# A fused two-block transformer kernel: moving operands at 128 instead of 256 modulo 512 bytes

## The reference

```python
def first_block(x, ...):
    z = rms_norm(h, attn_norm) @ w_in
    h = h + concat([gated_linear_attention(z), softmax_attention(z)]) @ w_out
    h = h + square(relu(rms_norm(h, mlp_norm) @ w_mlp_up)) @ w_mlp_down      # 1024 x 4096, 4096 x 1024
    return h + (p @ w_ple_proj) * sigmoid(rms_norm(h, ple_norm) @ w_ple_gate + b)

def second_block(x, ...):
    for i in range(2):
        h = rmsnorm(x, mix_norm[i])
        x = x + (pool_mixer(h) if i == 0 else chunk_attention(h))
        h = rmsnorm(x, ffn_norm[i])
        x = x + (silu(conv3(h @ w_gate[i])) * (h @ w_val[i])) @ w_out[i]     # 1024 x 2816 twice, 2816 x 1024
```

## The kernel before, in words

| tiles | before | after |
|---|---|---|
| X | 256 | 256 |
| AH (37,632 before), AL | 256 | 128 |
| RAW | 256 | 128 |
| WH (86,784 before), WL, stage, sq, rb, t2s | 256 | 256 |
| HH, HL (from 149,760 before) | 256 | 128 |
| OH, OL, OM, LM, pH, pL, cqb, v2, qTa, kTa | 256 | 256 |
| TH, TL, GH, GL | 448 | 448 |
| cst (with the identity) | 128 | 128 |

## Time and profile before

### The profile page before, as it was taken

How to read it: one execution, slowest core, us unless ns; L and a number is a source line. 1 busy time by engine, 2 the same in 40 slices (tenths; PEclk the granted TensorE clock), 3 DMA queues, 4 the chain that set the end, 5 groups by cost and what they waited for, 6 DMA issues and landing times.

```text
span 1613.5 us, 21756 instructions
## 1 busy us (share of the span) xinstructions
PE 1605.2 (99%) x9056; PEld 1357.5 (84%) x9056; DVE 1105.1 (68%) x1700; ACT 762.3 (47%) x1131; POOL 116.0 (7%) x102
## 2 busy tenths in 40 slices
PE   9999999999999999999999999999999999999999
PEld 7877878898989888888899898877777788899897
DVE  6798664696757657887587577546655877587575
ACT  5476445444443446654155244456565634155241
POOL 1300000011111100000000000312201200000000
PEclk9999999999999999999999999999999999999999
DMA  5310328356464521223222223322221213223222
GB/s 189 107 49 28 105 79 122 83 113 139 87 139 85 139 104 53 79 79 131 79 105 110 100 92 117 129 82 100 78 77 53 79 52 131 79 105 112 98 92 91
DMA packets 28065, 156.09 MB, mean 97 GB/s; under 512 B 3712, under 2 KB 5392, under 8 KB 12096
## 3 DMA queue, kind: packets, MB, share of 16 engines
q1 hardware_dynamic: 26352, 149.75, 25.8%
q0 software_dynamic: 1328, 4.86, 5.6%
q10 hardware_dynamic: 288, 0.10, 0.0%
HBM read 149.98 MB, written 4.72 MB: 96 GB/s over the span
## 4 chain that ended last, share of the span: by engine, by line
PE 95%; DVE 2%; ACT 1%; POOL 0%; DMA 0%; issue 0%; SPq 0%; DVEq 0%; ACTq 0%
PE bank L885 20%; PE bank L887 20%; PE bank L886 20%; PE bank L891 3%; PE bank L1494 3%; PE bank L1496 3%; PE bank L1495 3%; PE bank L893 3%; PE bank L892 3%; PE bank L1343 2%; PE bank L1345 2%; PE bank L1344 2%; PE bank L1611 1%; PE bank L1140 1%; PE bank L1621 1%; PE bank L1637 1%
## 5 line engine op out<-in xcount | busy, mean ns | idle before, releaser
L2152 DVE TENSOR_TENSOR WL<-RAW,WH 128x2048 fp32r<-128x2048 f32 (+2 forms) x90 | 199.6, 2224 | 129.8 <-ACT WH L1680 129.8
L885 PE MATMUL bank<-AH,WH 128*128 128x512 f32 (+1 forms) x718 | 283.2, 394 | 0.2 <-DVE X L2182 0.2
L887 PE MATMUL bank<-AH,WL 128*128 128x512 f32 (+1 forms) x718 | 279.7, 390 | 0.0
L886 PE MATMUL bank<-AL,WH 128*128 128x512 f32 (+1 forms) x718 | 279.6, 389 | 0.0
L885 PE MATMUL bank<-HH,WH 128*128 128x512 f32 x608 | 236.6, 389 | 0.0
L886 PE MATMUL bank<-HL,WH 128*128 128x512 f32 x608 | 236.6, 389 | 0.0
L887 PE MATMUL bank<-HH,WL 128*128 128x512 f32 x608 | 236.5, 389 | 0.0
L1680 ACT ACTIVATE WH<-RAW 128x2048 fp32r<-128x2048 f32 (+2 forms) x90 | 165.9, 1854 | 118.2 <-PE bank L887 81.5
L885 PEld LDWEIGHTS bank<-AH,WH 128*128 128x128 f32 (+1 forms) x718 | 134.4, 187 | 30.3 <-issue 2.4
L887 PEld LDWEIGHTS bank<-AH,WL 128*128 128x128 f32 (+1 forms) x718 | 134.4, 187 | 29.0
L886 PEld LDWEIGHTS bank<-AL,WH 128*128 128x128 f32 (+1 forms) x718 | 134.5, 187 | 28.0 <-issue 1.0
(11 more groups left out here) (389 smaller groups left out, 3262.9 us busy)
## 6 DMA issues: line engine op xcount, KB each, us to landing
RAW<-in_W SPq DMA_DIRECT2D x124, 1024.0 KB, 4.8
RAW<-in_W SPq DMA_DIRECT2D x9, 768.0 KB, 4.5
X<-in_XT SPq DMA_DIRECT2D x16, 256.0 KB, 5.3
ev_scratch<-ev POOLq DMA_DIRECT2D x16, 160.0 KB, 7.6
Gb<-ev_scratch SPq DMA_DIRECT2D x16, 128.0 KB, 4.3
Gb<-ev_scratch SPq DMA_DIRECT2D x16, 112.0 KB, 3.9
out<-X SPq DMA_DIRECT2D x7, 256.0 KB, 2.0
RAW<-in_W SPq DMA_DIRECT2D x2, 512.0 KB, 5.3
```

The costliest lines, as they stand in the source:

```text
L885: e.matmul(o, a, h, start=first, stop=False)
L886: e.matmul(o, a, l, start=False, stop=False)
L887: return e.matmul(o, c, h, start=False, stop=last)
L2152: e.tensor_tensor(k.WL[j][:, 0:n], k.RAW[RAW_OF[u]][:, 0:n], k.WH[j][:, 0:n].bitcast(F), SUB).then_inc(*WLO.mark(u))
```

## The change

Before AH the allocator now skips 384 bytes, so that AH and AL lie at 128 modulo 512, and so does RAW behind them; WH is brought back to 256 with `in_step`. The second stage's HH and HL start 128 bytes ahead of a place that is 256 modulo 512. The small tile `bps` moves into the gap behind `t1s`, and the `band` tiles keep their places relative to HH. TH, TL, GH and GL stay where they are. No instruction, wait or transfer is added, removed or moved in order.

```diff
+BEHIND = 384
@@ memory
     k.X = a.tile("X", [P, 8, S])
+    a.at += BEHIND
     k.AH = a.tile("AH", [P, 8, S], R)
     al_at = a.at
     k.AL = a.tile("AL", [P, 8, S], R)
     raw_at = a.at
     k.RAW = [a.tile(f"RAW{i}", [P, UE]) for i in range(NR)]
-    wh_at = a.at
+    wh_at = a.at = in_step(a.at)
     k.WH = [a.tile(f"WH{i}", [P, UE], R) for i in range(NW)]
...
-    a.at = base
+    hh_at = a.at = base + BEHIND - 512
     k.HH = [a.tile(f"HH{i}", [P, S], R) for i in range(NH)]
     k.HL = [a.tile(f"HL{i}", [P, S], R) for i in range(NH)]
     k.t1s = [a.tile(f"t1s{i}", [P, S + 2]) for i in range(2)]
+    k.bps = a.tile("bps", [P, 8])
     inner = a.at = in_step(a.at)
...
-    k.bps = a.tile("bps", [P, 8])
...
-              enumerate([base + 4 * S * 8] + [base + 4 * S * (NH + 8) + 4 * 4 * BW * i for i in range(3)])]
+              enumerate([hh_at + 4 * S * 8] + [hh_at + 4 * S * (NH + 8) + 4 * 4 * BW * i for i in range(3)])]
```

## The result

The changed kernel takes 1642.35 us (median of 4 runs, 1641.35 to 1644.11) against 1615.11 us before (median of 4): a ratio of 1.0164, 95% interval 1.0151 to 1.0176. It is slower, by 27 us; I had forecast 1579 us. The profiled execution took 1644.11 us, its span is 1641.9 us, and its mean granted clock is 0.997, against 1.000 before. It is the longest of the four; the spans of the others were 1639.2, 1639.3 and 1641.0 us.

What follows compares the result with a forecast made beforehand. TensorE, busy 99% of the span, bounds the kernel through its pitch per matmul. Gains of 33.4 + 6 = 39.4 us, less 8%, leave 36 us: 1615.2 - 36 = 1579 us, own range 1571 to 1588, whole range 1560 to 1617.

Steps and rivals of the forecast that it cites:

- (e): RAW at 128, so ScalarE and VectorE mix places within an instruction: 0, both engines having spare time.
- (f): Transfers into RAW start at another place: 0, ScalarE's waits for them not being on TensorE's path.
- The reading of the surplus: Weight load and moving stream conflict in SBUF: 32 cycles per matmul at the same place, at most 16 at 192 bytes.
- (a): 3978 matmuls of 512 columns with AH, AL, HH or HL moving: pitch 226.7 to 218.3 ns, gain 33.4 us.
- (b): 1104 matmuls of 256 columns with AH or AL moving: gain 6 us, 7.4 at most.
- (c): 672 value-projection matmuls with AH stationary, distance +128: taken as 0, between -4.5 and +4.5 us.
- (d): TH, TL, GH, GL, OH, OM, pH and cqb keep their distance: 0.
- The 8% taken off for VectorE: Deducted from TensorE's 39.4 us gain, as VectorE is nearly full in one stretch and 5% of the chain isn't TensorE.
- The slower one: Rival: longer conflict at -128, 560 cycles instead of 544; (a) costs +26.6 us, (b) +7.4, giving 1649 us; 14%.
- Its mechanism: Slower rival's reason: at -128 the faster moving stream starts behind the load, catches up and crosses it in full.
- The repetition rival: Places repeat every 128 bytes, so 384 equals 0: surplus stays 32 cycles, 1615 us; 13% together with the ports' rule.
- 73% for faster: Chance of a gain over 3.2 us: forecast case 48% plus the floor case 25%.

Runs made afterwards that it cites:

- the bench: Kernel of nothing but fp32r matmuls at many places, reference computation left out: 512 columns 226.8 ns at distance 0, 233.3 at 192; 256 columns 120.0 and 113.4.
- e2: Changed kernel with AH, AL, RAW, HH and HL at 448 modulo 512, weights still at 256: 1638.63 us, ratio 1.0146 to the kernel before.
- e4: Changed kernel with AH, AL, RAW, HH and HL at 0 modulo 512, weights at 256: 1616.26 us beside 1616.45 for the kernel before, ratio 1.0001.
- b3: Matmuls alone, other types, one repeated operand pair, and different preceding blocks: 512 columns bf16 215.8 or 215.9 ns, float32 429.2; 256 fp32r columns 113.3 or 117.8.

## Why the prediction was wrong

**What bounds the kernel.** Right. TensorE's pitch is the time; no other engine, wait or transfer took part in the result, and (e) and (f) were 0 as costed.

**The reading of the surplus.** Here it failed. From three sizes at distance 0 I had a surplus of 32 cycles, the same at 256, 384 and 512 columns, and concluded that it belongs to the weight load. Then I took TH's 16 cycles, measured with 256 columns at distance 192, as the upper end for distance -128 with 512: the sum's 5.0 ns in (a) is the middle between it and float32's 3.3. Neither row was a bound. With 256 columns a gain of 6.7 ns at distance 192 is real; with 512 the same distance loses 6.5 ns (226.8 against 233.3), and from 320 columns on no distance went under 13.3. At the change's own distance, 128, the surplus with 512 columns is 19.1 to 20.0 ns (232.4 and 233.3). Constant in the columns at one distance did not mean constant at another, and even at distance 0 three sizes were too few: 448 columns cost 16.0. And float32, at half the rate, has no trouble with any distance, so it says nothing of fp32r.

**(a)** was +23.1 us (11.8 + 11.3) in place of -33.4. **(b)** was 0.0 in place of -6; the bench at -128 gives 118.7 ns where TH's place gives 113.4. **(c)** was +3.0, within its bounds of 4.5 but not 0: the exchanged sides pay as the others do. **(d)** held for the places: 101 OH and OL matmuls are 227.1 ns apart in the trace after, though e2 showed that a tile can change its pitch without being moved. The 8% taken off for VectorE had no occasion to show itself.

**The rivals.** The slower one came true, at 14%, in sign and nearly in size: it priced (a) at +26.6 us for 560 cycles and the matmuls measured 233.3 ns at one place and 232.9 on average. Its +7.4 for the 256-column forms did not come, and (c) did, so 1649 became 1642. Its mechanism is not supported: it turned on the sign of -128, and +128 costs as much. So the price came out nearly right for a reason that did not hold, which is luck. The repetition rival was right in form and wrong in period: the pattern repeats every 256 bytes (e4), not every 128. Because 384 is 128 modulo 256, the change leaves the one good place; a step of 256 would have been free.

**The two rules.** The Trainium skill's page "TensorE: Matmul & The Clock Gate", under "Step-by-step: what each phase is for", gives the moving operand and the weights read ports of their own, and by that no distance can matter. bf16 and float32 agree with it in b3, to 0.1 ns; fp32r does not, by up to 11 ns. The same page's "Back-to-back issue gap" gives N/2.4 + 2.5 ns for a warm matmul alone, by estimate 215.8 ns for 512 columns; bf16 measured 215.8 and 215.9, fp32r 226.7 at the best.

**The numbers.** 73% for faster was too much for a quantity of which no row had either the distance or the size. An honest pair of ends for (a) would have reached as far above 13.3 ns as below.

What stays open is the cause beneath the distance. The surplus doesn't scale with the stationary columns, one displaced operand in four disturbs the whole triple, and two rhythms occur at the same places. A conflict between stream and load with some fixed slot in it would fit, but no run here shows it.

## What to carry to other kernels

For fp32r matmuls put moving and stationary operands at the same place modulo 256 bytes: with 512 columns that is the cheapest of all distances measured (240 equals it), and leaving it costs 1 to 3.5% of matmul time (5% at 4 bytes), here 1.6% of the kernel. For other sizes measure again: with 256 columns 192 was the best, with 448 columns 64; for bf16 and float32 the distances measured made no difference. When a row is carried to another size, check a third size at the same setting first, and where many settings are in question, one kernel with nothing but blocks of that instruction measures them all in one profile.

## What had not been expected of the hardware

- An fp32r matmul with 320 to 512 columns never took less than 13.3 ns over its columns at 2.4 GHz in any block measured (146.7 ns for 320, 226.7 for 512); bf16 needs 2.5 over.
- 4 bytes of distance (237.9 ns) are worse than 128, and 240 bytes (226.7) are as good as 0, while 16 (231.7) are not.
- Two steady rhythms for the same instructions, 113.3 and 117.8 ns with 256 columns at distance 192, lasting 189 matmuls in the bench and through all fast up units in e2, and 232.4 and 233.3 ns with 512 columns at distance 128. What chooses between them is open.
